# Projections between a norm's turns at five stage borders, and the overflow check ahead of the experts

## The reference, cut to what matters

```python
n2 = rms_norm(h, g_ffn); h = h + hier_moe(n2, ...)            # experts
gate = sigmoid(rms_norm(h, g_ple) @ w_ple_gate + b_ple_gate)  # norm "C"
h = h + gate * (p @ w_ple_proj)                               # does not need norm C
x = x + even_layer(rms_norm_2(x, norm_w[0]), ...)             # norm "D": q, k, v, gates of the mLSTM
x = x + hgrn2_layer(rms_norm_2(x, norm_w[1]), ...)            # norm "E": projections fx and ty
```

## Time and profile before

| what | value |
|---|---|
| median of 3 executions | 1990.47 us (1985.31 to 1991.77) |
| the profiled execution, its own time | 1988.54 us |
| its span, first to last instruction | 1986.7 us |
| PE busy | 1840.4 us (93%) |
| DVE, ACT, POOL busy | 762.0, 358.7, 98.0 us |
| DMA moved | 313.27 MB |

### The profile page before, as it was taken

The page is one execution under the profiler, slowest core; times in us unless marked ns, Lnnn a source line. Parts: engine busy times, 40 slices in busy tenths (PEclk is TensorE's granted clock), DMA queues, the critical chain, the costliest instruction groups (busy, mean ns, idle before and its releaser), DMA issues.

```text
span 1986.7 us, 17802 instructions
## 1 busy us (share of the span) xinstructions
PE 1840.4 (93%) x6758; PEld 906.1 (46%) x6758; DVE 762.0 (38%) x1430; ACT 358.7 (18%) x703; POOL 98.0 (5%) x133
## 2 busy tenths in 40 slices
PE   5999999996799999999979899999998889999986
PEld 3445554444333343333334354545565544545543
DVE  2323431124132232332332443535666533464473
ACT  1111111011000000000011121201433222243230
POOL 1200000000000000000010000011000000000000
PEclk9999999998899999999979899999799789999998
DMA  7212121216699999999912122122100022121001
GB/s 292 95 53 106 43 95 43 96 55 255 249 428 426 427 426 427 427 426 428 409 52 95 53 95 96 53 102 90 48 1 1 12 95 90 43 85 43 0 1 43
DMA packets 27945, 313.27 MB, mean 158 GB/s; under 512 B 3456, under 2 KB 3616, under 8 KB 10448
## 3 DMA queue, kind: packets, MB, share of 16 engines
q1 hardware_dynamic: 21168, 289.20, 35.5%
q0 software_dynamic: 6688, 22.88, 3.2%
HBM read 307.35 MB, written 4.19 MB: 157 GB/s over the span
## 4 chain that ended last, share of the span: by engine, by line
PE 73%; DVE 12%; DMA 10%; issue 2%; ACT 2%; POOL 1%; DVEq 0%; SPq 0%; POOLq 0%; ACTq 0%
PE ps L345 69%; DVE arena L979 6%; PE ps L348 4%; DMA wring<-in_w 4%; DMA arena<-in_w 4%; DMA HT<-in_w 2%; ACT arena L1816 1%; DVE arena L990 1%; DVE H L979 1%; DVE small L994 1%; DVE arena L1006 1%; DMA H<-in_x 1%; POOL small L2176 1%; DVE HT L1006 0%; DVE ps L979 0%
## 5 line engine op out<-in xcount | busy, mean ns | idle before, releaser
L345 PE MATMUL ps<-wring,HT 128*128 128x512 f32 (+1 forms) x1664 | 729.2, 595 | 8.2 <-DVE HT L1006 7.4
L345 PE MATMUL ps<-arena 128*128 128x64 f32 (+14 forms) x2232 | 453.4, 390 | 40.9 <-ACT arena L1816 13.3
L345 PEld LDWEIGHTS ps<-wring,HT 128*128 128x128 f32 x1664 | 313.3, 195 | 376.6 <-issue 371.5
L345 PEld LDWEIGHTS ps<-arena 128*128 128x128 f32 (+5 forms) x2232 | 252.2, 172 | 212.9 <-issue 199.5
L979 DVE TENSOR_TENSOR arena<-ps,arena 128x512 f32<-128x512 f32 (+1 forms) x157 | 102.3, 652 | 615.8 <-PE ps L345 456.2
L345 PE MATMUL ps<-wring,arena 128*64 128x512 f32 (+1 forms) x1056 | 320.2, 603 | 10.5 <-DMA wring<-in_w 5.3
L345 PE MATMUL ps<-HT,wring 128*128 128x512 f32 x608 | 273.5, 606 | 2.2 <-DVE HT L1006 2.2
L348 PE MATMUL ps<-con,arena 128*128 128x128 f32 (+2 forms) x850 | 135.1, 304 | 70.4 <-DVE arena L990 49.0
L345 PEld LDWEIGHTS ps<-wring,arena 128*64 128x64 f32 (+1 forms) x1056 | 111.4, 147 | 173.0 <-issue 170.0
L1816 ACT ACTIVATE arena<-ps 128x512 f32<-128x512 f32 (+4 forms) x151 | 76.5, 507 | 609.4 <-PE ps L348 353.5
L345 PEld LDWEIGHTS ps<-HT,wring 128*128 128x128 f32 x608 | 115.8, 194 | 143.5 <-issue 143.0
(11 more groups left out here) (76 smaller groups left out, 560.6 us busy)
## 6 DMA issues: line engine op xcount, KB each, us to landing
wring<-in_w SPq DMA_DIRECT2D x56, 2048.0 KB, 21.2
wring<-in_dense SPq DMA_DIRECT2D x39, 2048.0 KB, 8.4
arena<-in_w SPq DMA_DIRECT2D x27, 2048.0 KB, 22.1
HT<-in_w SPq DMA_DIRECT2D x13, 2048.0 KB, 22.2
arena<-in_rows POOLq DMA_DIRECT2D x34, 256.0 KB, 7.6
H<-in_x SPq DMA_DIRECT2D x4, 512.0 KB, 14.0
arena<-in_relb POOLq DMA_DIRECT2D x8, 256.0 KB, 9.2
n_scratch<-arena POOLq DMA_DIRECT2D x4, 512.0 KB, 3.0
```

The source lines that it names most:

```text
L345: return nc.tensor.matmul(o, l, r, start=start, stop=stop, skip_group_check=True)
```

## The change

- Entry: only the first 129 columns of `con` (identity and the exponent of the root) are loaded early, under a semaphore `ident`; `pcl` and the rest of `con` come after `w_k`. POOL starts the bias tables after its four roots. PE does three turns, then q for tiles 0 and 1, then turn A3, then q for 2 and 3.
- Row buffers: four instead of three, so the lists of rows on POOL shift, and all buffers of the scratch area move by 512 columns.
- The overflow check moves ahead of the experts on all five engines; SP does it after 7 expert loads. Its body restores the two slots that it uses. `ovd` is gone.
- The load and the transposes of `p` move into the experts, the latter ahead of the last combine.
- Gate: `w_pp` products first, one turn C after each tile, their results copied by ACT to `proj`; then `w_pg` by tile, with turns D0 and D1 after the tiles 2 and 3. The norm's sums begin as soon as a tile's combine is added. The sigmoids are 512 wide.
- mLSTM: `m_v` first, with turns D2 and D3 inside; then `if`, `m_q`, transposes, `cc`, `m_k`, `cols`.
- Recurrent layer: turns E0 and E1 inside `e2`; pair 0 takes its groups in the order 4 to 7, 0 to 3, with turns E2 and E3 after groups 4 and 6; the bound's small operations move ahead of the last tile's norm.

```diff
-                pe.wait_ge(S("con"), 16)
-                for i in range(4):
+                pe.wait_ge(S("ident"), 16)
+                for i in range(3):
                     turn("A", i)
                 w = weight("w_q")
                 for i in range(4):
                     turned("A", i)
                     used["w_q"] = tok(("q", i), w, i)
+                    if i == 1:
+                        turn("A", 3)
...
+                overflow_pe()
                 turn_rows(0)
...
+                v_ = pt.rearrange("t (a p k) -> t a k p", a=4, k=2)
+                pe.wait_ge(S("p"), 16)
+                for k in range(2):
+                    f = fill(("pT", k))
+                    for i in range(4):
+                        ins = tr(f.ap[:, i * 128:i * 128 + 128], v_[:, i, k, :])
+                    ins.then_inc(f.full, 1)
                 combine(NE // 2 - 1)
-                overflow_pe()
...
             def stage_c():
...
+                evacuated(("pT", 0), ("pT", 1))
                 w = weight("w_pp")
                 for i in range(4):
                     for h in range(2):
                         used["w_pp"] = tok(("pp", i, h), w, i, src=pT, n0=512 * h, nk=2, wide=1024)
+                    turn("C", i)
+                ws = [weight(f"w_pg{h}") for h in range(2)]
+                for i in range(4):
+                    turned("C", i)
+                    for h in range(2):
+                        used[f"w_pg{h}"] = tok(("pg", i, h), ws[h], i)
+                    if i > 1:
+                        turn("D", i - 2)
...
             def stage_d():
+                w = weight("m_v")
+                for i in range(4):
+                    turned("D", i)
+                    used["m_v"] = tok(("mv", i), w, i)
+                    if i in (0, 2):
+                        turn("D", 2 + i // 2)
+                wi = weight("n_if")
...
+                for n in range(2):
+                    used["n_if"] = feat(("cc", n), wi, 128 * n)
+                w = weight("m_k")
+                for c in range(4):
+                    used["m_k"] = feat(("m_k", c), w, c * 128)
...
+                    if not p and n > 3:
+                        turned("E", n - 4)
...
+                        if not p and n in (4, 6):
+                            turn("E", n // 2)
...
+GROUPS = [(4, 5, 6, 7, 0, 1, 2, 3)] + [tuple(range(8))] * 3
...
+                r = row("b_mv")
...
+                stat(3, *g)
+                values(0)
+                turned("D", 2)
+                values(1)
+                values(2)
                 turned("D", 3)
+                values(3)
...
-            sp.dma_start(pcl[:, :], T["pcl"]).then_inc(S("pcl"), 16)
-            sp.dma_start(con[:, :], T["con"]).then_inc(S("con"), 16)
+            sp.dma_start(con[:, 0:129], T["con"][:, 0:129]).then_inc(S("ident"), 16)
...
+            load("w_q")
+            load("w_k")
+            sp.dma_start(pcl[:, :], T["pcl"]).then_inc(S("pcl"), 16)
+            sp.dma_start(con[:, 129:], T["con"][:, 129:]).then_inc(S("con"), 16)
+            for key in ORDER_A[2:] + ORDER_B[:7]:
                 load(key)
             sp.wait_ge(S("oi"), 1)
             n = sp.value_load(oi[0:1, 16:17], min_val=0, max_val=NOV - 1)
```

More of the change, by code:

```diff
@@ L1087, in stage_a @@
                         turned("A", i - 1)
[L1088 to L1091 removed]
+                v.wait_ge(S("con"), 16)
                 def normed(z, go):
+                    if not go:
+                        m = row("misc")
+                        copy(gq, m[1][:, 0:128])
+                        row_done(m)
                     r = head_norm(z, sqA, 8, 64)
@@ L1102, in heads_out @@
                         copy(dst[:, :, i * 128:i * 128 + 128], f.ap.rearrange("p (a t) -> p a t", a=4), f)
-                biased("q", zq, row("b_q"))
+                r = row("b_q")
+                for i in range(4):
+                    f = full("q", i)
+                    tt(zq[:, i, :], f.ap, r[1], ADD, f)
+                    if i == 1:
+                        turned("A", 3)
+                row_done(r)
                 normed(zqf, 0)
@@ L1672, in group @@
                             row_done(rz)
+                        if not p and n in (4, 6):
+                            turned("E", n // 2)
                 rz = [0, 0]
@@ L1943, in stage_b @@
                 last[:] = before
+                rows_in(0)
+                for g in range(NE // 2):
+                    f = full("w1", g)
+                    act(hid[g % 2], f.ap, ACT.Sigmoid, "sg")
+                    f = full("hT", g)
+                    copy(hT[g % 2], f.ap.rearrange("p (k t) -> p k t", k=4), f)
+                    if g + 1 < NE // 2:
+                        rows_in(g + 1)
+                    if g > 1:
+                        full("cb", g - 2, 3, 1)
+                    f = full("y", g, 1)
+                    copy(ys[g % 2][:, 512:1024], f.ap, f)
@@ L1945, in stage_c, with square @@
+                f = full("pT", 0)
+                copy(pT[:, 0, :], f.ap, f)
             def stage_c():
-                heard("ovd")
-                for i in range(4):
-                    full("t", "BC"[i > 1], (i + 2) % 4, 1)
-                    if i < 2:
+                def square(nm, was, i):
+                    full("t", nm if i > 1 else was, (i + 2) % 4, 1)
+                    if nm == "C" and i < 2:
                         a.wait_ge(S(f"keep{i}"), 32)
                     stat(i)
-                    if i:
-                        turned("C", i - 1)
@@ L1954, in stage_c, with projected @@
-                turned("C", 3)
-                for h in range(2):
-                    freed(("pg", h, 3))
-                    g_ = gate[:, :, h * 512:h * 512 + 512]
-                    act(g_, g_, ACT.Sigmoid, "gs")
-                f = full("pT", 0)
-                copy(pT[:, 0, :], f.ap, f)
-                for i in range(4):
+                def projected(i):
+                    for h in range(2):
+                        f = full("pp", i, h)
+                        copy(proj[:, i, h * 512:h * 512 + 512], f.ap, f)
@@ new lines, in stage_c @@
+                for i in range(2):
+                    freed(("cb", NE // 2 - 1, i, 1))
+                    square("C", "B", i)
+                for i in range(4):
+                    projected(i)
+                    turned("C", i)
+                    if i < 2:
+                        freed(("cb", NE // 2 - 1, i + 2, 1))
+                        square("C", "B", i + 2)
+                for i in range(4):
+                    for h in range(2):
+                        freed(("pg", i, h))
+                        g_ = gate[:, i % 2, h * 512:h * 512 + 512]
+                        act(g_, g_, ACT.Sigmoid, "gs")
+                    if i > 1:
+                        turned("D", i - 2)
@@ L1975, in padded, with convolved @@
                     act(pads[x % 2][:, 3:515], f.ap, ACT.Identity, f, bias=PC(("b_mq", "b_mk")[x // 4])[:, c:c + 1])
-                padded(0)
-                for x in range(8):
-                    if x < 7 and x < 1:
-                        padded(x + 1)
+                heard("ab")
+                act(t16, t16, ACT.Exp, scale=-1.0)
+                act(t16, t16, ACT.Ln, "ln", bias=C("one"))
+                freed(("if", 3))
+                act(gates, gates, ACT.Sigmoid)
+                def convolved(x):
                     heard("cv")
@@ L1995, in stage_d @@
                 act(rb, rb, ACT.Exp, "rx")
+                padded(4)
+                padded(5)
+                for x in range(4, 8):
+                    convolved(x)
+                    if x < 6:
+                        padded(x + 2)
                 for h in range(4):
```

318 lines of the change are left out of this document (148 added, 170 removed).

## The result

The changed kernel takes **1943.45 us** (median of 4 runs, 1943.22 to 1943.72). The kernel before, on the same chip, takes 1987.89 (4 runs, 1984.45 to 1991.77). That is a ratio of 0.9776, 95% interval 0.9754 to 0.9798, and 44.4 us less. The forecast was 1940, inside a range of 1932 to 1957.

A forecast was written before the change was run, and what follows sets the result against it. PE was taken as the bound, so only its idle time (146 us) or lower clock could give time. Terms -7.8 + 0.9 - 36.5 + 3.9 - 10.5 = -50.0 from 1988.54 gave 1938.5, median forecast 1940 us, range 1932 to 1957.

The forecast's parts named there:

- Entry: Start of the kernel: q starts at 19.3 instead of 28.02, 7.8 us gained, bounds 2.7 and 8.9.
- The check: Overflow check ahead of the experts: 0.9 us lost, bounds 0 and 5.6, PE's price taken as DVE's 3.98 us.
- The experts: Expert stage: weight waits untouched by the change, and a gain made ahead of the expert loads is kept.
- Last combine to last value tile: Gate, norm D and m_v in one PE stream: 105.0 us instead of 141.5, 36.5 us gained.
- mLSTM: mLSTM projections: PE waits 5.8 us for the last convolutions, then starts cold; 3.9 us lost, bounds 1.4 and 4.6.
- the term of 3.2 us for cold starts that go: mLSTM projections: m_q and cc both began cold before; now only one stream follows `if`, 3.2 us gained.
- Recurrent entry: Recurrent layer's border, from e2 through eight groups: 76.1 us against 86.7, 10.5 us gained.
- The low bound of 1934: Whole kernel: total if the check is hidden, turns alone set the entry and there is no cold start.
- The norm's chain: First rival, at D and E: the norm's chain still sets the pace, +16 us, 1956 us; chance 0.14.
- the second rival: Fixed costs at their far ends: w_q late (+5.1) and PE's branch dear (+4.7), 1950 us; chance 0.14.
- The third: Rival, combine to m_v: turns strewn into the streams keep PE at its lower clock, 2045 us; chance 0.02.
- The fourth: Rival: little gain, as experts' DMA takes back the entry's gain and borders hide other waits, 1975 us; chance 0.04.

The follow-up runs named there:

- E0: Not a run: the first of the four PE turns at the recurrent layer's entry, which the change places inside that entry's first products; no measured time of its own.
- c1: Changed kernel with turns D2 and D3 both ahead of the first value tile, instead of inside the value tiles: 1955.39 us.
- b3: Changed kernel with the recurrent layer's entry put back (all turns E ahead of the value tiles, old order of weights and groups): 1956.99 us.
- b4: Changed kernel with the loads of pcl and the whole con early again, ahead of the first weights: 1944.93 us.
- c2: Changed kernel with all four turns A ahead of the first q tile, loads as changed: 1943.36 us.
- a3: Changed kernel with DVE's operations that make the overflow count moved ahead of its wait for the row lists' product: 1937.60 us.
- b2: Changed kernel with the edits of a3, a4 and b1 together: 1932.08 us.
- a4: Changed kernel with the table p loaded right behind the first gathers, into a free half of the norm's buffers: 1942.13 us.
- a2: Changed kernel with the overflow check and its skipped blocks left out on all five engines: 1941.38 us.
- b1: Changed kernel with the mLSTM's two cc products, ACT's activations of them and DVE's copies moved behind m_k and the convolutions: 1932.98 us.
- a1: Changed kernel run once more without any edit, for the spread: 1943.37 us.
- c3: Kernel before the change, with the overflow check and its blocks left out on all engines: 1980.78 us.

## Why the prediction was right, and where it was off

**What bounds the kernel.** Right: PE's idle time and its clock at the borders. c1 puts back half a border and b3 a whole one, at 12.0 and 13.6 us, with PE's idle time in the trace where the earlier trace rows has it.

**Entry.** Right in size: q at 19.05, forecast 19.3. Both bounds named there were nearly equal: w_q, issued at 4.61, landed 13.9 us later at 18.5, and the third turn ended at 19.26. b4 (loads, 3 us) and c2 (turns, 2.8 us) each take a third of it back alone. The gain is 8.9 and not 7.8 because the stream behind began less cold: 128 products and turn A3 took 56.6 us, where the products alone took 56.5 before. That none of it reached the experts is the first thing the prediction lacked: it took a gain ahead of the routing as kept.

**The check.** This is the step that failed, inside its bounds: "with DVE's price PE, DVE and ACT come out at 509.7: 0.9 us lost". It took PE's check as dear as DVE's, 3.98 us, "as the same code". PE's takes 6.5 us from the count to the first turn, and 3.45 of it stand bare: 3.4 us lost. The prediction also held that PE's check "isn't visible" and lies in the idle gap of 8.74 us. It was visible, in the lines of PE's sequencer: 5.87 us from 992.3, beside the last combine. With the load of the count ahead of it (0.9 us, from 991.4), the same sum gives 505.8 + 0.9 + 5.9 = 512.5, that is 3.7 us lost.

The Trainium skill ("Runtime: NRT & Kernel Launch", Instruction fetch mechanics) says that a taken branch out of the fetched window stalls; it gives no price. The traces agree: the branch ends 1.4 us after an instruction packet has landed, in eleven traces out of eleven, and a3 and b2 pay 3.4 and 3.5 us where that packet starts early. The sum of the move: 3.9 us saved behind the last combine, 3.4 to 3.8 spent ahead of the experts, so the move alone gave about nothing. For PE the old place was the free one, and for DVE the new one. a3 keeps the new place free for both, with another order in front of it.

**The experts.** Forecast 0, measured +1.4, from the larger waits for weights (a4). The stretch from 609 to 788, whose growth was named as a sign of being wrong, did not grow: PE waits 8.6 us there for weights, 9.1 before. That a gain ahead of the experts is kept through them holds by a2 (4.6 us, then 4.4).

**Last combine to last value tile.** Right: 104.1 us against 105.0 forecast, and 141.5 before. DVE did wait 5.5 us for the row b_mv, until 1082.0, but PE wanted turn D2 at 1080.5 and D3 at 1095.1, and waited for neither. The one wait is 0.8 us for ACT's copy of D3, forecast 0.75, and the 0.35 us forecast for D2 did not come.

**mLSTM.** Right in mechanism: a gap of 5.7 us (5.8 forecast), made by the chain that the prediction lists, and 2.5 us of half clock behind it (2.5). The stage lost 5.0 us and not 3.9, because the term of 3.2 us for cold starts that go was too large. Before, m_q lost 2.2 and cc 1.7 (57.2 and 15.4 us against 55.0 and 13.7 at the unit price); after, m_q still loses 2.1. So 1.9 was gained. b1 shows that the loss was avoidable: with the cc products behind m_k, PE has work while the last convolution runs.

**Recurrent entry.** -9.2 against -10.5. e2 begins colder than forecast (its first 24 records lose 2.7 us, 2.0 were put), and the two waits for E0 and E3 take 1.9 where 1.5 was put. b3, undoing the border alone, measures 10.5 from its own, colder start.

**The sum.** The forecast of 1940 is 3.5 us off, and part of that closeness is luck. The routing stage's clock, the attention's end and the dearer check cost 7.9 us that the prediction did not have, while the sparse attention and the later pairs, for which nothing was forecast, gave back 5.1. The low bound of 1934 isn't reached by the three terms that the prediction names for it (0.9, 1.1 and 2.5 us give 1935.5).

**The rivals.** The norm's chain did not set the pace: PE waited 0.8 us at D and 1.9 in the recurrent border. w_q was not late; PE's branch was dear, as the second rival had it, by 2.5 of its 4.7. The third, the clock in mixed streams: 1.00 from 1000 to 1104, with eight turns strewn in that take 1.05 us each. By the rule of the Trainium skill ("TensorE: Matmul & The Clock Gate", Part 4: PE-mode transpose) transposes do not engage the full clock; in company with products they did not lower it either. The clock fell elsewhere, in the narrow products of the routing, where no rival looked. The net of all clock terms is small (1.3 + 4.1 - 1.7 and most of -3.4), so it hardly shows in the total. The fourth had the entry's gain taken back by the experts' DMA. It was taken back, but ahead of the experts, by the clock and the check.

## What to carry to other kernels

Work that needs one tile of a norm belongs between the turns of that norm, and the last turn wants at least one chain's length of such work ahead of it: here two misplaced turns cost 12 us. The same holds for any chain over other engines: put the work that doesn't need it between its start and its first user, as b1 does with the cc products. A gain made ahead of a stage that waits on something else must be followed through it mark by mark before it's counted. Ahead of a branch or a semaphore that several engines read, put the few operations that feed it before the ones that wait, and read the branch's price on each engine by itself, from the sequencer's lines.

## What the runs showed of the hardware

The clock of PE makes the same work take different times, by more than most of the edits here. The stretch from the last transposes of the scores to the first turn E took 201.4 us in the changed kernel and 197.4 in c2, with DVE and ACT alike. The last stretch took 292.5 in a1 and 300.9 in a2. A start 3 us later went with the shorter of the two (b4 and c2).

In the kernel before, both groups of narrow products behind a wait in the routing stage ran at the full clock, and in c3, with the same order, the first of them. In all eleven profiles with the changed order the clock fell at or in the first, with the same PE instructions at the same distances in front of it for 62 us (the first traces of both kernels). Shifts of 3 us (b4, c2) don't change that. The groups stand at 465 to 470 us in the eleven and at 474 and 475 in the two, so no run separates the order from the time. What it hangs on is open.

A check that finds nothing to do has not the same price on every engine, nor at every place. PE's branch takes 5.4 to 6.5 us beside the gathers, 5.9 beside the expert loads, and 3.4 to 3.5 where it begins ahead of the gathers, and it ends 1.4 us after a packet of 16 KB of instructions has landed. On DVE the whole check took 4.0 in the kernel before.
